# A two-layer encoder trunk on one core: the maxima of the second attention's first block moved into the projection, the output projection's first tile spread over the last head pair, and three orders changed around the feed-forward layers

## What is computed

```python
h = concat([meta, x])                                  # 1040 tokens x 1024
h = h + neighbourhood_attention(rmsnorm(h)) @ w_o      # windows of 8x16 and the meta tokens
h = h + (silu(u @ w1) * (u @ w3)) @ w2                 # u = rmsnorm(h)
# layer 1: 16 query heads, 4 key/value heads of 64
q, k = rope(rmsnorm(q) * gain), rope(rmsnorm(k) * gain)
p = softmax(q @ k.T); h = h + (p @ v) @ w_o
h = h + (silu(u @ w1) * (u @ w3)) @ w2
out = rmsnorm(h)[meta:]
```

## Time and profile before

| | |
|---|---|
| median of 3 runs | 2728.22 us (2723.64 to 2732.25) |
| the profiled execution's own time | 2727.93 us |
| its span | 2725.8 us |
| PE busy | 2672.0 us, 98% of the span |
| DVE, ACT, POOL busy | 1503.1, 945.5 and 1536.8 us |
| mean granted TensorE clock | 0.994 |

### The profile page before, as it was taken

The page is one execution under the profiler, slowest core; times in us unless marked ns, Lnnn a source line. Parts: engine busy times, 40 slices in busy tenths (PEclk is TensorE's granted clock), DMA queues, the critical chain, the costliest instruction groups (busy, mean ns, idle before and its releaser), DMA issues.

```text
span 2725.8 us, 39814 instructions
## 1 busy us (share of the span) xinstructions
PE 2672.0 (98%) x14623; PEld 2203.8 (81%) x14623; DVE 1503.1 (55%) x1963; ACT 945.5 (35%) x1630; POOL 1536.8 (56%) x1291
## 2 busy tenths in 40 slices
PE   8999999899999999999999899999999999999998
PEld 7888888699999999999877545555677888888887
DVE  5444444437444444444778866767456445545545
ACT  4333334424222222223322556555232222222234
POOL 4665565446655555567244657665446556655571
PEclk9999999999999999999999999999999999999998
DMA  8222122421111111111243000001211111111111
GB/s 227 61 61 61 57 61 61 178 73 56 50 54 50 50 46 46 46 46 58 87 93 70 21 1 16 16 1 63 90 47 54 51 53 50 54 54 58 50 57 63
DMA packets 200468, 163.06 MB, mean 60 GB/s; under 512 B 19816, under 2 KB 182032, under 8 KB 200352
## 3 DMA queue, kind: packets, MB, share of 16 engines
q1 hardware_dynamic: 193728, 139.83, 17.9%
q10 hardware_dynamic: 6624, 21.68, 2.1%
HBM read 131.70 MB, written 24.51 MB: 57 GB/s over the span
## 4 chain that ended last, share of the span: by engine, by line
PE 92%; DVE 3%; issue 2%; DMA 1%; POOL 1%; SPq 1%; ACT 0%; ACTq 0%; DVEq 0%; POOLq 0%
PE PS L1002 30%; PE PS L1059 17%; PE PS L934 13%; PE PS L1204 9%; PE PS L1479 6%; PE PS L1493 5%; PE PS L1256 2%; PE PS L1292 2%; PE PS L1419 2%; PE PS L1232 2%; DMA wraw<-in_a_w_qkv 1%; DVE ssq L2053 1%; PE PS L1364 1%; PE PS L1270 1%; PE PS L1437 1%
## 5 line engine op out<-in xcount | busy, mean ns | idle before, releaser
L712 POOL TENSOR_TENSOR wl<-upraw,wh 128x512 fp32r<-128x512 f32 x212 | 284.4, 1344 | 270.4 <-ACT wh L1612 270.1
L686 POOL TENSOR_TENSOR wh<-wraw,ones 128x512 fp32r<-128x512 f32 x120 | 142.8, 1190 | 378.7 <-PE PS L934 199.2
L2106 DVE TENSOR_TENSOR h<-PS,h 128x1044 f32<-128x1044 f32 (+1 forms) x176 | 217.0, 1233 | 197.1 <-PE PS L1059 197.0
L1612 ACT ACTIVATE wh<-upraw 128x512 fp32r<-128x512 f32 x212 | 133.8, 631 | 498.9 <-POOL upraw L706 171.9
L1979 ACT ACTIVATE pf<-PS 128x512 f32<-128x512 f32 (+1 forms) x288 | 169.8, 594 | 161.1 <-PE PS L1479 159.9
L2558 DVE TENSOR_REDUCE nmx<-PS 128x1 fp32r<-128x1044 f32 x128 | 156.7, 1228 | 100.8 <-PE PS L1419 100.7
L689 POOL TENSOR_TENSOR wl<-wraw,wh 128x512 fp32r<-128x512 f32 x120 | 190.8, 1590 | 9.4
L712 POOL TENSOR_TENSOR wl<-wraw,wh 128x512 fp32r<-128x512 f32 x74 | 99.1, 1339 | 136.7 <-ACT wh L1612 135.1
L875 POOL TENSOR_TENSOR accp<-accp,pf 128x1024 f32<-128x1024 f32 x64 | 152.7, 2385 | 18.1 <-ACT pf L1979 17.1
L1842 ACT ACTIVATE pt<-PS 128x512 f32<-128x512 f32 x128 | 75.8, 592 | 240.8 <-PE PS L1256 234.2
L1493 PE MATMUL PS<-pf,vg 128*64 128x512 f32 x576 | 155.1, 617 | 0.0
(11 more groups left out here) (343 smaller groups left out, 7230.7 us busy)
## 6 DMA issues: line engine op xcount, KB each, us to landing
upraw<-in_ffn_w SPq DMA_DIRECT2D x166, 256.0 KB, 2.8
wraw<-in_ffn_w SPq DMA_DIRECT2D x98, 256.0 KB, 2.8
wraw<-in_a_w_qkv SPq DMA_DIRECT2D x48, 256.0 KB, 2.9
biasb<-bias_shifts SPq DMA_DIRECT2D x128, 72.0 KB, 2.5
h_spill<-h ACTq DMA_DIRECT2D x16, 522.0 KB, 4.5
h<-h_spill ACTq DMA_DIRECT2D x8, 522.0 KB, 7.4
h<-h_spill SPq DMA_DIRECT2D x8, 522.0 KB, 7.0
xt<-in_x SPq DMA_DIRECT2D x16, 256.0 KB, 7.5
```

Of the source, the lines that this page charges most:

```text
L712: nc.gpsimd.tensor_tensor(wlr[l][slot], rb[l][r], whr[l][slot].bitcast(F32), ALU.subtract).then_inc(s_wrd, 1)
L2106: nc.vector.tensor_tensor(out_, x, y, op_).then_inc(sem_, 1)
```

## The change

Five edits:

1. `O_FILL` is spread from the first filler of pair 7 to the last step, chunk 6 comes behind the last probs. SP issues the loads of chunks 0 to 3 one unit earlier, fetches weight units 50 and 51 ahead of chunks 4 to 6, and each chunk has its own semaphore.
2. At the end of the first feed-forward layer DVE leaves out the sums of squares 4 to 7 until all low parts are made; ACT has a ring of four squares. `stat(2)` comes behind both units of item 0, in banks 5 to 7, and item 1 waits for its reading only before its head sums. `zero_even` (the clearing of block 0's operands) moves behind the first `take_sums`.
3. ACT rounds the first two product weights (`first_two`) ahead of `silu(0)` and `block_hi(2)`, in both feed-forward layers.
4. Block 0's eight `tile_max` move into items 8 and 11, one behind each quarter of an item; item 9 waits for the fourth maximum. Its two `max_row` are plain float32 in banks 6 and 7, `v_by_key` uses banks 0 to 2. `lo_part` is spread over items 5 to 11.
5. The last item's `rope` moves into step 1 of block 0, the rounding of the identity into step 3.

```diff
-O_FILL = [14, 15, 16, 17, 19, 20, 22]
+O_FILL = [0, 4, 6, 11, 16, 22]
-L0_AT = [7, 7, 8, 8, 8]
+L0_AT = [5, 8, 10, 10, 11]
+MAX0_AT = {8: (0, 1, 2, 3), 11: (4, 5, 6, 7)}
+MAX0_SET = {8: 3, 11: 0}
+        STAT_AT = [D1, D1, 5, D1]
...
-            sp.wait_ge(s_un, U_WO[0])
+            sp.wait_ge(s_un, U_WO[0] - 1)
             for k in range(KC - 1):
+                if k == 4:
+                    sp.wait_ge(s_un, U_WO[0])
+                    fetch_chunk(U_WO[0] + 2, w_o[0], P)
                 sp.wait_ge(s_osp0, 32 * (k + 1))
-                sp.dma_start(uh[:, k, :].bitcast(F32), oh_spill[:, k, :]).then_inc(s_ox[k // 4], 16)
-                sp.dma_start(ul[:, k, :].bitcast(F32), ol_spill[:, k, :]).then_inc(s_ox[k // 4], 16)
+                sp.dma_start(uh[:, k, :].bitcast(F32), oh_spill[:, k, :]).then_inc(s_xl[k], 16)
+                sp.dma_start(ul[:, k, :].bitcast(F32), ol_spill[:, k, :]).then_inc(s_xl[k], 16)
-            fetch_wo(0, 1)
+            fetch_wo(0, 2)
...
+                if k != 2:
                     stat(k)
                 unit(n + 1, 1, set_, xh, xl, range(4, 8), False, True, l, KC * k)
+                if k == 2:
+                    stat(k)
...
             probs(NPAIR - 1, 8, VF * NPAIR)
+            o_filler(6)
             pv(NPAIR - 1, 4)
             o_filler(7)
...
+                if i == 9:
+                    pe.wait_ge(s_mr, 4)
                 for part in range(4):
...
+                    if i in MAX0_AT:
+                        if part == 0:
+                            pe.wait_ge(s_qsq, i)
+                            pe.wait_ge(s_gqh, 5)
+                            pe.wait_ge(s_gs1, 5)
+                            pe.wait_ge(s_gql, 1)
+                        tile_max(0, MAX0_AT[i][part], MAX0_SET[i])
...
-            for i in range(BT):
...
-                tile_max(0, i, 5 * (i % 2))
-                if 1 <= i <= 3:
-                    v_by_key(0, i - 1)
-                if i == 1:
-                    head_sums(ITEMS - 1, 3)
-                if i == 4:
-                    pe.wait_ge(s_idr, 1)
-                    pe.wait_ge(s_vgh, 3)
-                    max_row(0, 0)
-            pe.wait_ge(s_mset, 1)
-            max_row(0, 1)
+            pe.wait_ge(s_mt, 3 * (NG - 1))
+            max_row(0, 0)
+            max_row(0, 1)
+            for f in range(3):
+                v_by_key(0, f)
+            head_sums(ITEMS - 1, 3)
+            pe.wait_ge(s_z0, 17)
+            pe.wait_ge(s_gql, 5)
...
+                act.wait_ge(s_tl, 4 * l + 2 - l)
+                first_two(us, 1, 1)
                 act.wait_ge(s_df, gb + 2)
                 silu(0)
                 act.wait_ge(s_un, us - 1)
                 block_hi(2)
-                act.wait_ge(s_tl, 4 * l + 2)
...
-                        add_square(2 * l + 2, m - 1, sq_ffn[l])
-                add_square(2 * l + 2, KC - 1, sq_ffn[l])
+                        add_square(2 * l + 2, m - 1, sq_ffn[l], l or m <= 4)
+                add_square(2 * l + 2, KC - 1, sq_ffn[l], l)
                 if l == 0:
+                    for m in range(4, KC):
+                        sum_square(2, m, sqf0)
                     rsqrt(2, sqf0)
...
             for i in range(1, ITEMS):
                 g, c = divmod(i, 3)
+                maxima = MAX0_AT.get(i, ())
+                for tile in maxima[0:1]:
+                    take_max(0, tile, MAX0_SET[i])
                 take_sums(i - 1, 6)
+                if i == 1:
+                    zero_even()
                 if c == 0:
                     for step in range(5):
                         head_rsqrt(g - 1, step)
+                for tile in maxima[1:2]:
+                    take_max(0, tile, MAX0_SET[i])
                 if g and c:
                     scale_chunk(g - 1, 2 if c == 1 else 1)
+                for tile in maxima[2:]:
+                    take_max(0, tile, MAX0_SET[i])
                 rope(i - 1)
...
                     if n == 0:
                         if kt == 0:
                             take_sums(ITEMS - 1, 3)
+                        if kt == 1:
+                            rope(ITEMS - 1)
+                        if kt == 3:
+                            nc.vector.tensor_copy(ident_r[:, :], ident[:, :]).then_inc(s_idr, 1)
                         if 2 <= kt <= 6:
                             head_rsqrt(NG - 1, kt - 2)
```

More of the change, by code:

```diff
@@ L143, in build @@
         ssq = sb("ssq", [P, TP], F32)
+        nmx = sb("nmx", [P, BT], F32R)
         ident = sb("ident", [P, P], F32)
@@ L344, in build @@
         s_vt = sem("gqa_v_transposed")
-        s_xl = [sem(f"x_left_half{i}_loaded") for i in range(9)]
+        s_xl = [sem(f"x_left_half{i}_then_o_parts{i}_loaded") for i in range(9)]
         s_xca = sem("x_bank_read_by_act")
@@ L957, in dense_of_new_u @@
                 unit(n, 0, set_, xh, xl, range(0, 4), True, False, l, KC * k)
-                stat(k)
+                if k != 2:
+                    stat(k)
                 unit(n + 1, 1, set_, xh, xl, range(4, 8), False, True, l, KC * k)
+                if k == 2:
+                    stat(k)
             def spread(set_, w, x, l=0):
@@ L1425, in max_row @@
                 pe.wait_ge(s_mr, BT * n + 4 * (e + 1))
+                if n == 1 and e == 0:
+                    pe.wait_ge(s_idr, 1)
                 for i in range(4):
+                    if n == 0:
+                        mm = nc.tensor.matmul(PS[:, 6 + e, P * i:P * i + P],
+                                              nmx[:, 4 * e + i:4 * e + i + 1].bitcast(F32).to_broadcast([P, P]),
+                                              ident[:, :], start=True, stop=True)
+                        continue
                     mm = nc.tensor.matmul(PS[:, 4, P * i:P * i + P],
@@ L1578, in squares @@
                 act.wait_ge(sem_, need)
[L1579 to L1582, removed]
+                t, ring = TOK[k // 3], 4 if k == 2 else 2
+                if m >= ring:
+                    act.wait_ge(s_acc, (KC - 1) * (k - 1) + m - ring + 1)
+                if k == 2 and m == 2:
+                    act.wait_ge(s_gr, 2 * FIT)
+                nc.scalar.activation(square_of(k, m, buf)[:, 0:t], h[:, m, 0:t], ACT.Square).then_inc(s_sq, 1)
                 if k == 4:
@@ L1630, in gate, with first_two @@
                     silu(b)
-                def first_quad(n, i, last, s, l22, l11, l21, l12):
+                def first_two(n, l22, l11):
                     r = ROLES[0][0]
-                    o = [op(l, last, j) for j in range(8)]
                     loaded(r[A22], l22)
@@ L1638, in first_quad, with rest_of_first_quad @@
                     hi(n, 2, r[A11])
+                def rest_of_first_quad(n, i, last, s, l21, l12):
+                    r = ROLES[0][0]
+                    o = [op(l, last, j) for j in range(8)]
                     if l == 0:
@@ L1931, in set_max @@
                 act.wait_ge(s_mrow, 2 * n + e + 1)
-                nc.scalar.activation(qx[g % 2][64:65, q0:q0 + QB], PS[64:65, 4, :], ACT.Copy).then_inc(s_mset, 1)
+                nc.scalar.activation(qx[g % 2][64:65, q0:q0 + QB], PS[64:65, 4 if n else 6 + e, :], ACT.Copy).then_inc(s_mset, 1)
             def hi_part(g, par, n):
@@ L1996, in _ @@
                         hi_part(0, 0, n)
-            for f in range(3):
-                v_copy(0, 0, f)
             act.wait_ge(s_z0, 17)
@@ L2001, in _ @@
             set_max(0, 1)
+            for f in range(3):
+                v_copy(0, 0, f)
             for s in range(NG * STEPS):
@@ L2425, in _, with zero_even @@
             nc.vector.memset(v_gq[64:96, :], 1.0).then_inc(s_vx, 1)
[L2426 to L2438 removed]
+            dve.wait_ge(s_vx, 4)
+            def zero_even():
+                nc.vector.memset(y_gq[:, :], 0.0).then_inc(s_z0, 1)
+                dve.wait_ge(s_z0, 1)
+                for a in range(0, QW, QB):
+                    nc.vector.tensor_copy(qx[0][64:P, a:a + QB], y_gq[64:P, :]).then_inc(s_z0, 1)
+                dve.wait_ge(s_hsp, 2 * 16 * KC)
+                for a in range(0, TW, TW // 3):
+                    nc.vector.tensor_copy(kx[0][64:P, a:a + TW // 3], y_gq[64:P, 0:TW // 3]).then_inc(s_z0, 1)
+                nc.vector.tensor_copy(kx[0][0:64, T:TW], y_gq[0:64, 0:TW - T]).then_inc(s_z0, 1)
+                nc.vector.tensor_copy(ks[0][:, TP:TW], y_gq[:, 0:TW - TP]).then_inc(s_z0, 1)
+                dve.wait_ge(s_z0, 14)
+                for a, n in ((0, QB), (QB, QB), (GRID, META)):
+                    nc.vector.tensor_scalar(kx[0][64:65, a:a + n], y_gq[64:65, 0:n], 1.0, None,
+                                            ALU.add).then_inc(s_z0, 1)
             def take_sums(i, bank):
@@ L2597, in o_part @@
                                         ALU.mult).then_inc(s_gob, 1)
-            for i in range(BT):
-                take_max(0, i, 5 * (i % 2))
-            rope(ITEMS - 1)
             for n in range(NBP * NG):
```

90 lines of the change are left out of this document (38 added, 52 removed).

## The result

The changed kernel takes **2732.92 us** in the median of 20 runs (2726.98 to 2739.38), the kernel before 2727.85 on the same chips: ratio **1.0021**, 95% interval 1.0014 to 1.0027. By the ratio that is 5.7 us more; the forecast was 2717.0, and its range ended at 2724. So the difference is small, under the 0.3% named in the prediction, but the interval leaves out 1: it is a loss, and the forecast is missed by some 16 us.

What follows compares the result with a forecast made beforehand. PE, busy 98% of the span, was taken as the bound, leaving only its waits and the slow clock behind them. 5.8 + 2.0 + 4.4 - 0.2 - 1.1 = 10.9 us off 2727.93 gave 2717.0 us, range 2710 to 2724.

Steps and rivals of the forecast that it cites:

- 1.1 us more: Second attention's start and block 0: 1.0 gained ahead, 0.9 by the table, 3.0 lost; bounds 2.5 less to 4 more.
- `rope(10)` (3.7) and itself (1.2): Ahead of block 0: DVE's rotation takes 3.7 us and `lo_part(4)` 1.2, within a 6.6 us stretch behind item 11.
- The table is loaded early: Ahead of block 0: idle ACT loads its exp table before its first exp, gaining 0.9 us.
- I take 3.0: Block 0: DVE's added `rope(11)` and identity copy cost 3.0 us; work sum gave 1.1, step count 3.0 to 3.9.
- 4.4 us less: Second feed-forward layer: early weight rounding starts the second product 4.9 us earlier, less 0.5 for the third weight; bounds 3 to 6.5.
- the two sums and the low part took 4.9 us: Second feed-forward layer: POOL readies the second product weight in 4.9 us, by 2069.9, leaving PE a 1.7 us wait.
- second rival: Second product: POOL stays slow beside DVE, three operations take 9.6 us for 4.9; total 2721.5; chance 0.23 shared with block 0's rival.
- the bound "0 to 1": First feed-forward layer: the early weight rounding costs 0.2 us more, between 0 and 1, since `silu(0)` waits longer.
- The wait that replaces the old one: Ahead of item 3: PE waits 3.2 us for unit 282's weight split, with one clock fall taken at 2.0 us.
- first rival: Items' new wait is short or leaves the clock up: 2715 without the fall, 2713.5 with half the wait; chance 0.22.
- the bound of 7.2: Sums of squares and items: upper bound of the gain, 7.2 us if no new wait comes; lower bound 0.5.
- other-side rival: Items: weights come late in every item, each of nine waiting 2 us or more; 2725 to 2737 us; chance 0.05.

Runs made afterwards that it cites:

- E5: Changed kernel with `nmx` allocated last in the second attention, so every other tensor has its old address: 2725.86 us, ratio 0.9997 to the kernel before.
- E9: E5 with POOL's eleven zero copies held until DVE has `lo_part(4)`: 2721.27 us, ratio 0.9979 to the kernel before.
- E7: E5 with the last item's `rope` again ahead of block 0's loop: 2721.32 us, ratio 0.9985 to the kernel before.
- E4: E3 plus ACT's early rounding of the first two product weights in both feed-forward layers: 2719.21 us, ratio 0.9965 to the kernel before.
- E3: Kernel before with only the moved fillers and spill loads and most of the sums-of-squares change, `nmx` where it was: 2718.35 us, ratio 0.9963.
- E2: Kernel before with only an unused 32-byte-a-partition tensor behind `ssq`: 2737.02 us, ratio 1.0031.
- E12: Kernel before with an unused 32-byte tensor ahead of all tensors, shifting weights and moving operands alike: 2726.62 us, ratio 1.0004.
- E6: E5 with DVE's `lo_part(4)` one item earlier, in item 10: 2719.33 us, ratio 0.9974 to the kernel before.
- E8: E5 with the moves of E6 and E7 together: 2726.85 us, ratio 0.9999 to the kernel before.
- E1: Changed kernel with an unused 32-byte-a-partition tensor behind `nmx`: 2727.18 us, ratio 0.9998 to the kernel before.
- E11: E6 plus earlier `lo_part` calls, identity copy on ACT, item 3's first weight half loaded earlier, 64 bytes more scratch: 2712.74 us, ratio 0.9950 to the kernel before.

## Why the prediction was wrong, point by point

- **A term that isn't there: +6.5 us.** The forecast prices each edit by engines and waits, and has none for the line that moves `nmx`. Its part of the sum is the changed kernel's ratio less E5's (1.0021 and 0.9997), good to some 3 us; the loop's own trace has 6.9. This alone turns no change into a loss.
- **Edits 4 and 5: "1.1 us more", measured 8.7.** Three steps of it. (a) "`rope(10)` (3.7) and itself (1.2)" took 5.7 and 1.95, beside POOL's zero copies; shown by E9. So 1.8 us were lost ahead of block 0, not 1.0 gained. (b) "The table is loaded early", 0.9: it wasn't. The pattern in the trace of before was taken for a rule; what decides the place was not tried. (c) "I take 3.0" for block 0, less the 0.9 of the table: 5.6. The step-by-step count was of the right kind, but its `rope(11)` was 3.7 long and became 7.0. The sum also had no fall of the clock there; two came, behind the waits of 4.46 and 2.99. Undoing that move alone (E7) took 4.6 of 6.0 us back.
- **Edit 3: "4.4 us less", measured nothing (E4 against E3: 0.5 us more, within the noise).** The first product did start 4.3 us earlier. The step that failed is "the two sums and the low part took 4.9 us": they took 8.1, the second product waited 4.94 instead of 1.7, and the clock fell again. In other runs with edit 3 the three took 6.9 (E5) and the second product waited 3.6, and the column of the first products lies between 0.7 us lost and 2.6 gained, never near 4.4. This is the second rival in its place, and nearly its price (9.6 for 8.1); that DVE is what slows POOL here is read from the traces, no run tested it at this place. In the first layer the bound "0 to 1" was passed: 1.6. I had the rows for both outcomes and took the favourable one, though the nearest row is the one with DVE as busy as it would be.
- **Edit 1: right.** 5.8 forecast, 5.5 measured, against the one profile of before; PE's waits of over 0.15 us in pair 7 fell from 9.3 to 3.9 us in all, as forecast (3 to 4). In E2 and E12, whose pairs run the same code as the kernel before, that section took 1.7 to 1.9 us more, with a lower clock in it, so the gain over many executions may be larger.
- **Edit 2: right in its mechanism; the size is partly chance.** The wait that replaces the old one came at item 3 with 2.93 us. The clock didn't fall behind it in the changed kernel, E6 and E7, and did in E5, behind 2.89 us (granted 0.58 from 1372 to 1380 us, where the changed kernel had 1.00), and in E8 and E9. So the term lies between 1.2 and 4.7 us; I gave 2.0 and the first rival 4.0. A slip on the way: the parts named for the bound of 7.2 (4.5, 0.4 and 2.7) add up to 7.6; the arrival at 1377.1, on which the rest stands, is 7.2 earlier.
- **The other-side rival**, late weights in every item, did not happen; the loss came by another way.

By the ratios the whole divides into edits 1 and 2 -10.1 us, edit 3 +0.5, edits 4 and 5 +8.7, addresses +6.5. Each is the difference of two neighbours in the row before, E3, E4, E5, changed kernel, so they must add up to the whole and don't prove one another.

## What to carry to other kernels

Before pricing a move, list what it does to the *addresses* of everything allocated behind it; where TensorE is the bound and 98% busy, an unused tensor of 32 bytes can cost more than an edit gains. Price VectorE's and GpSimd's work at its slow duration wherever both have work, on both engines, and ask which of the two the critical chain goes through. And don't add up two moves that live on the same idle time: E6 and E7 won 6.3 and 3.3 us alone and nothing together.

## What the hardware showed that I had not expected

- **The distance between weights and moving operand.** A 512-column fp32r matmul at full clock took 389 ns where the moving tile lies a multiple of 128 bytes from the weights' tile (`ghs` to `wh` in the kernel before; `oh` to `wh` in E1 and E11), and 393 to 394 where `ghs` and `gls` lie 32 bytes further (the changed kernel, E2). An odd multiple of 64 gave two answers: 394 to 396 for `oh` (before: 394, E12: 396), but 390 to 392 for `ghs` and `gls` in E1, and E1's pass lies between the others. Moving both alike changes nothing (E12). Between starts it is 227 ns for `ghs` before and 233 in the changed kernel. `uh` and `ul` took 392 to 394 everywhere; their rows are 4176 bytes long, no multiple of 64, so they have no common distance. That the distance counts is shown by E2 against E12; that multiples of 128 bytes are the fast case is read from these layouts only, with addresses worked out from the order and sizes of the allocations, and what sets the time at other distances stays open.
- **The clock is no function of the wait's length.** It stayed up behind waits of 2.93 us (changed kernel) and 2.12 (E6) at the same place where it fell behind 2.89 (E5, granted 0.58), 2.44 (E8, 0.79 from 1375 to 1383 us) and 2.28 (E9, 0.79 from 1371 to 1379). At the second product it stayed at 1.00 from 2069 to 2075 us behind a wait of 3.59 in E7, and was 0.50 from 2072.5 to 2078.5 behind one of 3.62 in E8. In E11 it fell at one of 1.38 (granted 0.79 from 1436 to 1444 us). Waits up to 1.61 had looked safe.
- **DVE's small copy beside POOL.** `ident_r`, 128x128 from one SBUF input, took 0.20 us in the changed kernel with POOL idle beside it, 1.06 before beside POOL's casts, and 2.33 in E6, where POOL was summing beside it.
